# One-hot products without a step for the first expert of a mixture-of-experts block

## The reference, cut to what matters

```
h = rmsnorm(x, norm_ffn_g)
gp, gi = top_k(softmax(t @ w_group_router + b), 1)        # 1 of 4 groups
ew, ei = top_k(softmax(in_group), 2)                      # 2 of its 8 experts
weights = gp * ew / sum(ew);  eid = gi * 8 + ei
for e in range(32):
    hid = silu(t @ w_exp_gate[e]) * (t @ w_exp_up[e])     # 1024 -> 256
    out += combine[:, e] * (hid @ w_exp_down[e])          # 256 -> 1024
```

## Time and profile before

| | us |
|---|---|
| median of 3 runs | 883.54 (881.21 to 883.55) |
| the profiled execution | 883.49 |
| its span | 881.7 |
| PE busy | 803.0 (91%) |
| PEld busy | 654.9 (74%) |
| DVE busy | 354.5 (40%) |
| ACT busy | 241.3 (27%) |
| POOL busy | 292.3 (33%) |

### The profile page before, as it was taken

One profiled execution on the slowest core, in us unless ns is written; L12 is line 12 of the kernel. 1 busy time (PEld: TensorE's weight loads), 2 busy tenths in 40 slices (PEclk: granted clock), 3 DMA queues, 4 the chain that ended last, 5 costly groups with the idle time before them and its releaser, 6 DMA issues.

```text
span 881.7 us, 14886 instructions
## 1 busy us (share of the span) xinstructions
PE 803.0 (91%) x5813; PEld 654.9 (74%) x5813; DVE 354.5 (40%) x756; ACT 241.3 (27%) x418; POOL 292.3 (33%) x263
## 2 busy tenths in 40 slices
PE   5999999899899979999996998998999999987793
PEld 4888798788788857788885877897777777765551
DVE  6478760563663761336513512442111212121115
ACT  4333242112311756422213445410111111110012
POOL 3823444422430243044342353241333333332110
PEclk9999999999999999999998999977999999999998
DMA  9745504202210340464494374573999999999946
GB/s 255 140 102 107 110 12 96 48 1 49 49 41 9 74 118 7 90 163 124 96 257 76 70 218 159 199 283 132 369 393 382 394 393 386 389 386 376 396 186 248
DMA packets 71438, 162.77 MB, mean 185 GB/s; under 512 B 18834, under 2 KB 44258, under 8 KB 63192
## 3 DMA queue, kind: packets, MB, share of 16 engines
q1 hardware_dynamic: 63920, 150.66, 53.7%
q0 software_dynamic: 5472, 9.82, 3.3%
q10 hardware_dynamic: 1992, 1.55, 0.8%
HBM read 157.31 MB, written 13.04 MB: 193 GB/s over the span
## 4 chain that ended last, share of the span: by engine, by line
PE 59%; DMA 22%; DVE 8%; issue 4%; ACT 3%; POOL 2%; SPq 1%; DVEq 0%; POOLq 0%; ACTq 0%
PE bank L1015 15%; DMA arena<-in_w_exp_up 12%; PE bank L1022 11%; PE bank L1024 11%; PE bank L1023 10%; DMA ring<-in_w_exp_up 8%; PE bank L1359 4%; PE bank L1369 2%; PE bank L1316 2%; DMA ring<-in_w_cq 1%; DVE arena L1749 1%; PE bank L1346 1%; PE bank L1225 1%; DMA arena<-y_half 1%; ACT w_high L1434 1%
## 5 line engine op out<-in xcount | busy, mean ns | idle before, releaser
L1022 PE MATMUL bank<-h_hi,w_high 128*128 128x512 f32 x296 | 124.0, 419 | 2.3 <-DVEq L561 2.0
L835 POOL TENSOR_TENSOR ring_low<-ring,w_high 128x2048 fp32r<-128x2048 f32 (+1 forms) x16 | 71.5, 4469 | 149.9 <-ACT w_high L1434 149.8
L1023 PE MATMUL bank<-h_lo,w_high 128*128 128x512 f32 x296 | 117.0, 395 | 0.0
L1359 PEld LDWEIGHTS bank<-arena,hT 128*64 128x64 f32 x1728 | 97.5, 137 | 24.5 <-issue 24.5
L1359 PE MATMUL bank<-arena,hT 128*64 128x128 f32 x1728 | 101.2, 275 | 7.8 <-DMA arena<-in_w_exp_up 6.9
L835 POOL TENSOR_TENSOR w_low<-ring,w_high 128x2048 fp32r<-128x2048 f32 x14 | 64.4, 4600 | 78.9 <-ACT w_high L1434 76.9
L2019 DVE SCALAR_TENSOR_TENSOR rt<-rt,bank 128x128 f32<-128x128 f32 x32 | 9.2, 287 | 176.6 <-ACT rt L1646 176.6
L1434 ACT ACTIVATE w_high<-ring 128x2048 fp32r<-128x2048 f32 (+1 forms) x32 | 58.8, 1838 | 66.5 <-PE bank L1024 31.1
L1022 PEld LDWEIGHTS bank<-h_hi,w_high 128*128 128x128 f32 x296 | 56.6, 191 | 15.2 <-DVEq L561 2.3
L1024 PE MATMUL bank<-h_hi,ring_low 128*128 128x512 f32 x168 | 67.1, 399 | 0.0
L1023 PEld LDWEIGHTS bank<-h_lo,w_high 128*128 128x128 f32 x296 | 56.6, 191 | 9.7
(11 more groups left out here) (311 smaller groups left out, 1436.4 us busy)
## 6 DMA issues: line engine op xcount, KB each, us to landing
arena<-in_w_exp_gate SPq DMA_DIRECT2D x27, 1024.0 KB, 13.4
arena<-in_w_exp_up SPq DMA_DIRECT2D x27, 1024.0 KB, 16.6
arena<-in_w_exp_down SPq DMA_DIRECT2D x27, 1024.0 KB, 18.8
ring<-in_w_in SPq DMA_DIRECT2D x33, 512.0 KB, 6.6
ring<-in_w_exp_gate SPq DMA_DIRECT2D x5, 1024.0 KB, 14.1
ring<-in_w_exp_up SPq DMA_DIRECT2D x5, 1024.0 KB, 17.0
ring<-in_w_exp_down SPq DMA_DIRECT2D x5, 1024.0 KB, 19.7
xres<-in_x SPq DMA_DIRECT2D x8, 512.0 KB, 7.1
```

The lines of the kernel that those rows point to most:

```text
L835: after(pool.tensor_tensor(low, full, high, ALU.subtract), w_lo)
L1022: pe.matmul(o, l_hi, r_hi, start=(n == 0), stop=False)
L1023: pe.matmul(o, l_hi, r_lo, start=False, stop=False)
L1359: ins = pe.matmul(bank[CAP * half:CAP * half + CAP, 1, P * n:P * n + P], xgT[:, x, kk, :], w[:, kk, P * half:P * half + P], start=(kk == 0 ...
```

## The change

Three edits. The stationary operand of g0 takes 128 neighbouring words instead of every eighth. With that, row k * 128 + p of the turned tokens lies at partition p, piece k, so expert 0's gate and up matrices are loaded in the layout "(k p) f -> p k f": partition p holds the rows p, 128 + p, and so on, eight runs of 1 KB. And the gains are taken from `gcol["ffn"]`, which has that order, for the first expert only. The first expert's down matrix, all other experts, the order of the jobs and the order of the requests stay as they are; the request for buffer 4 (the fifth) right behind `("co", 3, 1)` is in both kernels.

```
             def load_part(b, i):
-                sp.dma_start(expert_parts(b)[i], expert_sources(b)[i]).then_inc(...)
+                source = expert_sources(b)[i]
+                if b == 0 and i < 2:
+                    source = (w_exp_gate, w_exp_up)[i][0, 0].rearrange("(k p) f -> p k f", p=P)
+                sp.dma_start(expert_parts(b)[i], source).then_inc(...)
...
                     for kk in range(KD):
-                        ins = pe.matmul(o[:, CAP * kk:CAP * kk + CAP], normed_row[t].rearrange("p (d k) -> p k d", k=KD)[:, kk, :], first_at[:, t, :], ...)
+                        ins = pe.matmul(o[:, CAP * kk:CAP * kk + CAP], normed_row[t][:, P * kk:P * kk + P], first_at[:, t, :], ...)
...
+            first_gain_slots = gcol["ffn"].rearrange("p (k o) -> p k o", o=1).to_broadcast([P, KD, CAP])
+
-            def turned_by_gains(x):
-                return tt(xgT[:, x, :, :], bank[:, 0, :].rearrange("p (k s) -> p k s", k=KD), gain_slots, ALU.mult)
+            def turned_by_gains(x, gains=gain_slots):
+                return tt(xgT[:, x, :, :], bank[:, 0, :].rearrange("p (k s) -> p k s", k=KD), gains, ALU.mult)
...
-                    after(turned_by_gains(0), turned_sb)
+                    after(turned_by_gains(0, first_gain_slots), turned_sb)
```

More of the change, by code:

```diff
@@ L723, in load_part @@
             def load_part(b, i):
-                sp.dma_start(expert_parts(b)[i], expert_sources(b)[i]).then_inc(down_loaded[b] if i == 2 else w_loaded[b], 16)
+                source = expert_sources(b)[i]
+                if b == 0 and i < 2:
+                    source = (w_exp_gate, w_exp_up)[i][0, 0].rearrange("(k p) f -> p k f", p=P)
+                sp.dma_start(expert_parts(b)[i], source).then_inc(down_loaded[b] if i == 2 else w_loaded[b], 16)
             for n, c in enumerate(chunks):
@@ L1315, in emit @@
                     for kk in range(KD):
-                        ins = pe.matmul(o[:, CAP * kk:CAP * kk + CAP], normed_row[t].rearrange("p (d k) -> p k d", k=KD)[:, kk, :], first_at[:, t, :],
+                        ins = pe.matmul(o[:, CAP * kk:CAP * kk + CAP], normed_row[t][:, P * kk:P * kk + P], first_at[:, t, :],
                                         start=(t == 0 and kk == 0), stop=(t == NT - 1), skip_group_check=True)
```

## The result

The changed kernel takes 873.94 us (median of 4 runs, 872.26 to 874.10) against 883.17 before (median of 4 as well). The ratio is 0.9896, 95% interval 0.9876 to 0.9915: 9.2 us faster. The forecast was 876.6 with a range of 871.5 to 881.5. The profiled execution took 873.83 us, span 872.0.

A forecast was written before the change was run, and what follows sets the result against it. The experts' weight stream, and the TensorE chain before its start, were taken to bound the kernel. From 883.49 us, 7.5 won on the products (between 5.6 and 10.0) and 0.6 lost on the loads gave 876.6, range 871.5 to 881.5.

The forecast's parts named there:

- The bound: Expert weight stream fills the DMA engines and starts after the first expert's products (611.08); time won earlier reaches the end.
- Group one: First of four groups of 16 one-hot products, at full clock: 3.63 to 1.87 us, gain 1.76.
- group three: Third group of 16 one-hot products, after the fillers raise the clock: 3.87 to 1.87 us, gain 2.0.
- group two: Second group of 16 one-hot products, before the fillers, at half clock: 3.83 to 3.7 us, gain 0.13.
- group four: Fourth group of 16 one-hot products: 4.00 to 3.7 us at half clock, or 1.87 if the clock stays up.
- Rival B: TensorE's clock doesn't fall at 584.1 at all: products gain 13.5 us, time about 870.6; chance 0.08.
- A: The forecast case: products gain 5.6 to 10.0 us, loads lose 0 to 1.0, 873.5 to 878.9; chance 0.66.
- rival C: The clock comes back too late, only behind group three: gain 3.8 us, time 880.3; chance 0.10.
- The loss: Expert 0's gate and up transfers in 1 KB pieces, ahead of w_cq without cover: 0.6 us more.
- D: Expert 0's 1 KB pieces move at 221 GB/s: 4.4 us lost, time 880.4; chance 0.06.
- E: Pieces 128 KB apart pull expert 0's early transfer to 153 GB/s: 8.6 us lost, time 884.6; chance 0.04.
- F: Stepped load isn't what paced the products, or something else gates expert 0: 883 to 884 us; chance 0.06.

The follow-up runs named there:

- e11: Changed kernel with expert 0's three transfers asked for only once the first w_cq chunk has landed (SP waits for it); 873.66 us, ratio 0.9891.
- e3: Changed kernel with expert 0's three transfers asked for right behind the first w_cq chunk's request; 868.01 us, ratio 0.9839.
- e12: e11 plus e9's two fillers and seven more before the first turning of the x tiles; 866.53 us, ratio 0.9827.
- e2: Changed kernel with the stepped operand back and the 1 KB pieces kept; 884.05 us, ratio 1.0028.
- e7: Changed kernel with the stationary operand read with a step of two words in all four groups; 875.29 us, one run.
- e8: Changed kernel with the stationary operand read with a step of four words in all four groups; 884.67 us, one run.
- e9: Changed kernel with two filler products of 256 columns before the last tile's router products; 872.48 us, ratio 0.9895.
- e13: Kernel before, with the stepped operand, plus e9's two fillers before the last tile's router products; 882.54 us, ratio 1.0006.
- e4: Kernel before with expert 0's three transfers asked for right behind the first w_cq chunk's request; 879.10 us, ratio 0.9960.

## Why the prediction was right, and where it was off

The bound was right: the first request and the end moved together in every kernel run, with 268.7 to 271.8 us between them. That spread of 3.1 us is also how far a single profile can be trusted for the whole time.

The direct gains were right in size. Group one won 1.90 us (I had 1.76), the router products 1.65 (1.45), group three 2.06 (2.0). The single load was not as I said (192 ns, not near 140), but the sum didn't rest on it: it went by the groups of 36 and 128 columns, and the groups at full clock took 1.73 to 1.94 us where I had 1.87. At half clock I had 3.7, and e11 has 3.47 and 3.61.

The term that was mis-sized is the clock. I had 7.5 us for the products, from bounds of 5.6 and 10.0; the profile gives 11.8, outside both. Two choices made the difference. I let the clock fall at 584.1 as before, and it fell some 3 us later, so that group two won 1.39 and not 0.13. And I took a value between "falls again behind group three" and "stays up"; it stayed up, and group four (2.06), the list (0.79), the fillers with the gap (1.16) and the first expert (0.66) won all of it. Rival B, no fall at 584.1, had 13.5; the case lies between A's upper end and B, and I gave B only 0.08. e11 shows that the low end was real too: with the same operand, another moment of arrival gave 28.3 us instead of 20.2, a gain of 3.8 us, as much as in rival C.

The loss was under-sized. The w_cq wait grew by 1.1 us, not 0.6, and the first one-hot group came 1.66 us later. w_cq was in use 0.83 us later (its request had gone out 0.23 sooner), 0.66 was regained on w_ck's products (7.78 to 7.12), 1.6 lost on the products at 539, and 0.2 regained behind them. The chain of waits at 539, before and after:

```profile
538.89 2.02 PE bank L1015 x16
```

```profile
539.12 3.63 PE bank L1018 x16
542.76 0.90 PE bank L1276 x8
543.66 1.79 PE bank L1018 x16
```

The clock was half there for some 3.5 us. No row of before told of that, and it is not the price of the 1 KB pieces as such: e3 has the pieces too, behind w_cq, and 2.02 us there. In all fourteen profiles it goes with w_ck's first products: where they took 7.4 us or less, those near 539 took 3.3 to 3.7 (nine profiles, e11 and e12 too), and where they took 7.8 or more, 2.0 (five). What ties the two together is not shown.

The two errors have opposite signs: 4.3 us more won, 1.1 more lost, and 0.5 more behind the first request, which together leave the time 2.7 us under the forecast. That it fell well inside the range, with a gain outside my bounds, is partly luck. Of the rivals, D and E (the loads at 221 or 153 GB/s) are excluded by e2, F by e7 and e8.

What stays open: why the clock falls at 587 in the changed kernel and at 580 in e11 for the same instructions in the same order. The traces show only that it does, and that it did not fall in the two profiles (e9, e12) that had fillers in the 0.7 us gap and an unstepped operand. The mean clock of the whole span fits that in every run: 0.980 to 0.982 in the five of e9, 0.975 to 0.978 in the four of the changed kernel.

## What to carry to other kernels

Where the clock is full, an f32 stationary operand should be read with a step of at most two words (192 and 196 ns a load against 329 and 335); the layout of the weights that meet it can be chosen to fit, and pays for it with shorter runs. Look at what the cheaper operand does to the clock and not only to its own instructions: some 4.5 of the 11.8 us won stood in the rows of other products, and 3.4 of the rest in groups two and four, which only a full clock makes cheap (e11). Ask also of each early transfer what is queued behind it: expert 0's weights were needed 150 us after they were asked for, and stood in front of a chunk that an engine was waiting for.

## What the runs showed of the hardware that I had not expected

At full clock a step of two f32 words costs next to nothing (196 against 192 ns a load), one of four already the full price (329). At half clock the load without a step takes 333 ns, as long as a stepped one.

TensorE at 100% busy for 20 us can be at half clock all the time (e13), and it is the same with unstepped 64-column products once the clock is down (e11, 18 us).

Behind two requests of 1 KB pieces the next one takes SP longer: 4.77 us for expert 0's down transfer, 0.44 before, and 4.38 in e3 against 0.43 in e4. SP still had time before w_cq. Before and after:

```profile
444.64 0.44 SPq L724 DMA_DIRECT2D arena<-in_w_exp_down  x1
```

```profile
443.95 0.58 SPq L727 DMA_DIRECT2D arena<-in_w_exp_up  x1
444.57 4.77 SPq L727 DMA_DIRECT2D arena<-in_w_exp_down  x1
449.38 5.09 SPq L743 DMA_DIRECT2D ring<-in_w_ck  x4
459.70 1.27 SPq L743 DMA_DIRECT2D ring<-in_w_cq  x2
```
